# Two stacked transformer blocks on one core: the additions after the first down-projection in another order, and the low parts of the mixers' outputs 128 bytes further

## The chip, the cores and the metric
The kernel runs on one core of a Trainium2 chip. The metric is the device time in microseconds of one execution. Before the change the median of three runs is 984.97 us (984.92 to 984.98).

## The reference, cut to what matters
A sequence of 256 tokens of width 1024 goes through three layers in float32. In each, `h = h + mixer(rmsnorm(h))`, then `h = h + mlp(rmsnorm(h))`:

```
block 1, layer 0: mixer_ab  (attention on chosen keys | gated linear attention) -> 1024 columns, @ w_out_ab
                  mlp: square(relu(n @ w_up)) @ w_down,   w_up 1024x4096, w_down 4096x1024
block 1, layer 1: mixer_c   (stick-breaking attention, 8 heads of 128) -> 1024 columns, @ w_out_c
                  mlp of the same shapes
block 2:          16 meta tokens ahead of the 256; two gated branches, merged @ w_out;
                  gelu(a) * v of a convolved up-projection (2 x 2816 columns), @ w_down
```

rmsnorm divides each token's row by its root mean square and multiplies by a gain per column.

## The kernel before, in words
**Products in two parts.** Every large product is made of three matmuls on TensorE (helper `mm3`, lines 665 to 667): high x high, high x low, low x high. The high part is the value rounded to float32r, the low part is what is left. In the profile's names `whi`, `wlo` are the parts of a weight tile, `nhl` holds both parts of the normed tokens, `chi`, `clo` those of a mixer's output (`catT` in the code), `f`, `g`, `e` the areas with the parts of the three hidden layers, `mhi`, `mlo` those of block 2's merged branches and later of its normed tokens (`MG`). In a row as `bank<-whi,chi` the first name is the operand that is streamed through the array, the second is the one that is loaded into it.

**Weight tiles.** The weights come as 156 tiles, most of 128 x 2048 float32 (1 MB), in the order of use. For each tile i four steps run: SyncE issues its DMA into `raw` (slot i mod 3) when the low part of tile i-3 is made; ScalarE makes `whi` (line 1186, `hi(i)`) when the last matmul that read tile i-3 has ended; VectorE makes `wlo` (line 1750, `lo(i)`), for some tiles together with GpSimd (line 2422), each one half; then the matmuls may read it. Around the end of the first down-projection (tiles 35 to 50, `DOWN[0]` = 35) the tiles from 50 on are wholly VectorE's. Tiles 51 and 52 are the first two of the next layer's projection (`C0` = 51).

**Order of work.** Each engine has its own program, written out by hand in one order, with semaphores between the engines. An engine that waits lets nothing of its own program past.

**A projection back to tokens** (`out_tok`; s = 0 and 2 for the mixers, s = 1 and 3 for the first two MLPs) fills four PSUM banks: j = 2*tt + c, where tt is the half of the tokens and c the half of the columns. The loaded operand is the mixer's output or the hidden layer, the streamed one the weights, 512 columns a matmul. In the last tile the banks are finished one after the other in the order 0, 2, 1, 3, six matmuls each; ahead of bank 3 TensorE does `half_turn(t, 0)`: it transposes columns 0 to 511 of `h` (eight transposes, line 693), for which it waits until banks 0 and 2 have been added into `h`. VectorE's `add_out(s, j)` adds bank j into `h` once bank j is full; for s = 1 it is line 2035, since the MLP's row scale is applied there. Before the change VectorE first makes every low part up to tile 52 and then runs `out_h`: adds banks 0, 2, 1, makes the low parts of the transposed `h` (`half_turn`, line 1758, four instructions, after ScalarE's high parts, line 1194), adds bank 3. The next projection's first matmul needs the first of these four.

**Places in SBUF.** Tensors lie one behind the other in each partition, each rounded up to whole lines of 128 bytes: `raw`, `whi`, `wlo` (three each), `h`, `nhl`, `xn`, `clo`, `vec`, `cst`, `tri_sb`, small ones, and then the areas `a`, `f`, `g`, `c`, `b`, `e`, which share one room. `chi` and `mhi` lie on `xn`, `mlo` on `clo`. `xn` takes 8320 bytes, 32.5 times 256, so `clo` and `mlo` start 128 bytes off `chi` and `mhi` modulo 256. `whi`, `wlo`, `h`, `nhl`, `chi` start at the same place modulo 256 as one another; the high and the low part inside `f`, `g` and `e` do so too. `o_xn` and `o_clo` are the addresses of `xn` and `clo`, `place[0]` is the next free one.

Of the kernel before, what the change touches and what calls it, by code (L numbers as in the profile page):

```python
# [54 lines left out]
LINE = 128  # L55
# [169 lines left out]
UP, DOWN = (19, 67), (35, 83)  # L225
# [178 lines left out]
def block_kernel(nc, W, V, C, DL, CM, TRI, X, MT, WG, GP, OUT):  # L404
    ctx = ExitStack()
    with ctx:
# [3 lines left out]
        place = [base]  # L410
# [5 lines left out]
        def sb(name, n, dt=F32):  # L416
            off = place[0]
            place[0] += whole_lines(4 * n)
            return at(name, n, off, dt)
# [34 lines left out]
        o_xn = place[0]  # L454
        xn_ = sb("xn", 8 * N2)
        xn = xn_[:, 0:2 * D].rearrange("p (t n) -> p t n", t=2)
        o_clo = place[0]
        clo_ = sb("clo", 8 * S, F32R)
        place[0] = o_clo + whole_lines(8 * N2 * 4)
        catT = Pair(at("chi", 8 * S, o_xn, F32R), clo_).view("p (k t) -> p k t", k=8)  # L460
# [1276 lines left out]
        def vector_program(dve):  # L1737
# [3 lines left out]
            def lo(i):  # L1741
                j, m = i % NSLOT, cuts[i]
                if i < 2:
                    for c in range(4):
                        on.wait_ge(*s_hi01.at(i, c))
                        s = slice(c * 512, c * 512 + 512)
                        dve.tensor_tensor(wlo[j][:, s], raw[j][:, s], whi[j][:, s].bitcast(F32), ALU.subtract).then_inc(s_lo01.up(i, c))  # L1747
                    return
                on.wait_ge(*s_hi.at(i))
                dve.tensor_tensor(wlo[j][:, 0:m], raw[j][:, 0:m], whi[j][:, 0:m].bitcast(F32), ALU.subtract).then_inc(s_lod.up(i))  # L1750

            def evac_turn(t, q, dst):
                u = use["tr", t, q]
                on.wait_ge(*s_nhi.at(t, 2 * q + 1))
                for kk in range(2):
                    k = 2 * q + kk
                    o = dst[:, k, :]
                    dve.scalar_tensor_tensor(out=o.lo, in0=u.t[:, kk * 256:kk * 256 + 256], scalar=vcol(GAIN[t], k),  # L1758
                                             in1=o.hi.bitcast(F32), op0=ALU.mult,
                                             op1=ALU.subtract).then_inc(s_nlo.up(t, q) if kk == 0 else u.free if t < 4 else s_nodd.up(q))  # L1760

            def half_turn(t, c):
                for q in (2 * c, 2 * c + 1):
                    evac_turn(t, q, nTa if t < 4 else nT2[:, :, META:L2])
# [261 lines left out]
            def add_out(s, j, factor=None):  # L2026
                u = use["out", s, j]
                tt, c = j // 2, j % 2
                o = h[:, tt, c * 512:c * 512 + 512]
                on.wait_ge(*u.done(0 if j < 3 else (4, 16, 4, 16)[s] - 1))  # L2030
                if factor is None:
                    dve.tensor_tensor(o, o, u.t[:, :], ALU.add).then_inc(u.free)
                else:
                    on.wait_ge(*s_stat.at(factor, 2))
                    dve.scalar_tensor_tensor(out=o, in0=u.t[:, :], scalar=stats[factor][3][:, tt:tt + 1], in1=o,
                                             op0=ALU.mult, op1=ALU.add).then_inc(u.free)

            def out_h(s, factor, turn):
                for j in (0, 2, 1):
                    add_out(s, j, factor)  # L2040
                if turn:
                    half_turn(turn, 0)
                add_out(s, 3, factor)

            def mlp(l, t):
                def rest(m):
                    o, x = FFP[l][:, m * 512:m * 512 + 512], SQR[l][m % 2]
                    on.wait_ge(*s_ffhi.at(l, m))
                    dve.tensor_tensor(x, x, x, ALU.mult).then_inc(own.up())
                    on.wait_ge(*own.last())  # L2050
                    dve.tensor_tensor(o.lo, x, o.hi.bitcast(F32), ALU.subtract).then_inc(s_fflo.up(l, m))

                def joined(m, c):
                    u = use["up", l, m, c]
                    on.wait_ge(*s_half.at(l, m, c))
                    dve.tensor_tensor(SQR[l][m % 2][:, c * 256:c * 256 + 256], u.t[:, 0:256], HALVES[l][:, c * 256:c * 256 + 256],
                                      ALU.add).then_inc(u.free)

                for m in range(16):
                    if m:  # L2060
                        joined(m - 1, 1)
                    lo(UP[l] + m + 2)
                    if m == 0:
                        half_turn(t, 1)
                    joined(m, 0)
                    if m:
                        rest(m - 1)
                    if l == 1 and m == 6:
                        on.wait_ge(*s_mr.at(0))
                        dve.tensor_scalar(mnorm, meta, small[0:META, 9:10], None, ALU.mult).then_inc(s_mn.up(0))  # L2070
                joined(15, 1)
                rest(15)
# [4 lines left out]
                lo(OUT_AB + it + 2)  # L2077
            out_h(0, None, 1)
            mlp(0, 1)
            for it in range(16):  # L2080
                lo(DOWN[0] + it + 2)
            out_h(1, 1, 2)

# [397 lines left out]
        @block.vector  # L2483
        def _(eng):
            vector_program(eng)
# [124 lines left out]
```

## Time and profile before
| | |
|---|---|
| median of three runs | 984.97 us |
| profiled execution | 984.89 us |
| its span, first to last instruction | 983.1 us |
| TensorE (PE) busy | 971.7 us, 99% |
| VectorE (DVE) busy | 611.0 us, 62% |
| ScalarE (ACT) busy | 553.4 us, 56% |
| GpSimd (POOL) busy | 130.3 us, 13% |
| granted TensorE clock, mean | 0.998 |

PE counts a matmul from its start to its modelled end, and matmuls overlap, so two kernels may both show PE at 99% and still put their matmuls out at another pace: the distance from one matmul's start to the next is what counts. PEld is the load of the stationary operand, which runs beside the matmul ahead of it.

### The profile page before, as it was taken

What the parts mean: (1) busy time and instruction counts of PE and PEld (TensorE: products, weight loads), DVE (VectorE), ACT (ScalarE), POOL (GpSimd) and SP (SyncE); (2) the same over time, 40 slices, a digit from 0 to 9 for tenths busy, and PEclk for the clock granted to TensorE, in tenths of its full rate; (3) what the DMA queues carried; (4) which work ended last, traced back from release to release, by engine and by line L of the source; (5) the groups of instructions that cost most, each with busy time, mean ns of one, the idle gap of its engine ahead of it and who ended that gap; (6) DMA issues with size and microseconds to landing.
All of it is one profiled execution on the core that took longest, in us unless ns stands there. A gap on an engine that the chain in (4) does not pass through costs nothing.

```text
span 983.1 us, 14080 instructions
## 1 busy us (share of the span) xinstructions
PE 971.7 (99%) x5806; PEld 858.0 (87%) x5806; DVE 611.0 (62%) x894; ACT 553.4 (56%) x832; POOL 130.3 (13%) x44
## 2 busy tenths in 40 slices
PE   9999999999999999999999999999999999999997
PEld 7888888888888788888888888899999999999885
DVE  4997956777312554547777312376547689888643
ACT  6676347666433577846766433544454587665532
POOL 0011041000665000011000666300000000000000
PEclk9999999999999999999999999999999999999999
DMA  8454224555555543335545555464443535555541
GB/s 335 175 178 165 86 86 172 191 195 176 195 186 196 190 167 134 129 133 177 207 171 198 184 178 211 142 215 153 153 166 130 214 118 205 185 198 175 188 155 43
DMA packets 24804, 168.46 MB, mean 171 GB/s; under 512 B 2781, under 2 KB 3092, under 8 KB 4900
## 3 DMA queue, kind: packets, MB, share of 16 engines
q1 hardware_dynamic: 24452, 167.22, 47.2%
q8 instruction: 46, 0.75, 0.3%
q10 hardware_dynamic: 288, 0.33, 0.1%
q14 instruction: 18, 0.15, 0.1%
HBM read 166.49 MB, written 1.05 MB: 170 GB/s over the span
## 4 chain that ended last, share of the span: by engine, by line
PE 95%; ACT 2%; DVE 1%; DMA 1%; issue 0%; SPq 0%; DVEq 0%; ACTq 0%
PE bank L665 23%; PE bank L666 23%; PE bank L667 23%; PE bank L747 12%; PE bank L751 6%; PE bank L883 2%; PE bank L693 1%; DMA raw<-w_stream 1%; ACT whi L1186 1%; DVE wlo L1750 0%; PE bank L851 0%; PE bank L900 0%; PE bank L1094 0%; PE bank L993 0%; PE bank L1078 0%
## 5 line engine op out<-in xcount | busy, mean ns | idle before, releaser
L1750 DVE TENSOR_TENSOR wlo<-raw,whi 128x2048 fp32r<-128x2048 f32 (+2 forms) x152 | 310.7, 2045 | 266.0 <-ACT whi L1186 265.8
L1186 ACT ACTIVATE whi<-raw 128x2048 fp32r<-128x2048 f32 (+1 forms) x154 | 293.0, 1903 | 151.7 <-PE bank L667 148.9
L2422 POOL TENSOR_TENSOR wlo<-raw,whi 128x1024 fp32r<-128x1024 f32 (+1 forms) x37 | 129.1, 3493 | 496.0 <-ACT whi L1186 488.6
L747 PE MATMUL bank<-nhl,whi 128*128 128x512 f32 x512 | 130.4, 395 | 0.0
L667 PE MATMUL bank<-mhi,wlo 128*128 128x258 f32 x384 | 108.9, 284 | 0.0
L665 PE MATMUL bank<-mhi,whi 128*128 128x258 f32 x384 | 108.7, 283 | 0.0
L747 PEld LDWEIGHTS bank<-nhl,whi 128*128 128x128 f32 x512 | 92.2, 189 | 18.7 <-DVE nhl L1758 1.6
L666 PE MATMUL bank<-mlo,whi 128*128 128x258 f32 x384 | 108.3, 282 | 0.0
L665 PE MATMUL bank<-nhl,whi 128*128 128x258 f32 (+3 forms) x320 | 92.9, 290 | 0.0
L666 PE MATMUL bank<-nhl,whi 128*128 128x258 f32 (+3 forms) x320 | 91.3, 285 | 0.0
L667 PE MATMUL bank<-nhl,wlo 128*128 128x258 f32 (+3 forms) x320 | 90.5, 283 | 0.0
L665 PE MATMUL bank<-whi,nhl 128*128 128x512 f32 x192 | 76.9, 400 | 0.6 <-DVE wlo L1747 0.6
L667 PE MATMUL bank<-whi,nhl 128*128 128x512 f32 x192 | 74.9, 390 | 0.0
L666 PE MATMUL bank<-wlo,nhl 128*128 128x512 f32 x192 | 74.8, 390 | 0.0
L751 PEld LDWEIGHTS bank<-nhl,wlo 128*128 128x128 f32 x512 | 69.8, 190 | 5.0
L666 PEld LDWEIGHTS bank<-mlo,whi 128*128 128x128 f32 x384 | 72.8, 190 | 0.0
L667 PEld LDWEIGHTS bank<-mhi,wlo 128*128 128x128 f32 x384 | 72.5, 189 | 0.0
L665 PEld LDWEIGHTS bank<-mhi,whi 128*128 128x128 f32 x384 | 72.4, 189 | 0.1
L751 PE MATMUL bank<-nhl,wlo 128*128 128x256 f32 x512 | 71.4, 282 | 0.0
L665 PEld LDWEIGHTS bank<-nhl,whi 128*128 128x128 f32 (+1 forms) x320 | 60.4, 189 | 3.1 <-issue 2.9
L666 PEld LDWEIGHTS bank<-nhl,whi 128*128 128x128 f32 (+1 forms) x320 | 60.0, 188 | 0.2
L667 PEld LDWEIGHTS bank<-nhl,wlo 128*128 128x128 f32 (+1 forms) x320 | 60.1, 188 | 0.0
(298 smaller groups left out, 1757.9 us busy)
## 6 DMA issues: line engine op xcount, KB each, us to landing
raw<-w_stream SPq DMA_DIRECT2D x154, 1024.0 KB, 4.8
cst<-consts SPq DMA_DIRECT2D x1, 1200.0 KB, 11.6
h<-x_rows SPq DMA_DIRECT2D x4, 256.0 KB, 5.4
raw<-w_stream SPq DMA_DIRECT2D x2, 512.0 KB, 6.5
out_rows<-e SPq DMA_DIRECT2D x4, 256.0 KB, 2.1
e<-g_post SPq DMA_DIRECT2D x1, 512.0 KB, 3.7
raw<-w_stream SPq DMA_DIRECT2D x1, 352.0 KB, 9.5
b<-consts_x SPq DMA_DIRECT2D x1, 272.0 KB
```

What stands on the lines that cost most here:

```text
L665: pe.matmul(out, lhsT.hi, rhs.hi, start=start, stop=False)
L666: pe.matmul(out, lhsT.hi, rhs.lo, start=False, stop=False)
L667: return pe.matmul(out, lhsT.lo, rhs.hi, start=False, stop=stop)
L693: x = pe.transpose(u.t[:, kk * 256 + tt * P:kk * 256 + tt * P + P], h[:, tt, k * P:k * P + P], ident)
L747: return pe.matmul(us[c].t[:, :], w[:, k, c * P:c * P + P].hi, nboth[:, k, :], start=k == 0, stop=k == 7)
L751: pe.matmul(us[c].t[:, 0:256], w[:, k, c * P:c * P + P].lo, nTa[:, k, :].hi, start=False, stop=False)
L883: x = pe.matmul(u.t[:, i * P:i * P + P], kx, qx, start=True, stop=True)
L1186: act.activation(whi[j][:, 0:n], raw[j][:, 0:n], ACT.Copy).then_inc(s_hi.up(i))
L1750: dve.tensor_tensor(wlo[j][:, 0:m], raw[j][:, 0:m], whi[j][:, 0:m].bitcast(F32), ALU.subtract).then_inc(s_lod.up(i))
L2422: pool.tensor_tensor(wlo[j][:, m:n], raw[j][:, m:n], whi[j][:, m:n].bitcast(F32), ALU.subtract).then_inc(s_lop.up(i))
```

## The change
There are two edits. First, whole lines are added ahead of `clo` so that it lies at the same place modulo 256 as `xn` (and `chi`); `clo`, `mlo` and everything placed behind them move up by 128 bytes. Second, in VectorE's program, after the low part of tile 51, banks 0 and 2 are added first, then comes the low part of tile 52 (`DOWN[0] + 17`), then bank 1, the four low parts of the transposed `h`, and bank 3. No instruction is added or removed on any engine.

```
-        o_clo = place[0]
+        o_clo = place[0] = place[0] + (place[0] - o_xn) % (2 * LINE)
...
-            for it in range(16):
+            for it in range(15):
                 lo(DOWN[0] + it + 2)
-            out_h(1, 1, 2)
+            add_out(1, 0, 1)
+            add_out(1, 2, 1)
+            lo(DOWN[0] + 17)
+            add_out(1, 1, 1)
+            half_turn(2, 0)
+            add_out(1, 3, 1)
```

## Rows read from the trace of the kernel before

**Rows 1.** The page's parts 1 and 2: TensorE's busy time, its granted clock by slice.
```profile
PE 971.7 (99%) x5806; PEld 858.0 (87%) x5806; DVE 611.0 (62%) x894; ACT 553.4 (56%) x832; POOL 130.3 (13%) x44
...
PEclk9999999999999999999999999999999999999999
```
**Rows 2.** The view of waits from 330 us on, TensorE: us in total, times, longest.
```profile
PE bank L693 <- DVE h L2035: 1.1, 1, 1.1
```
**Rows 3.** The timeline, end of the first down-projection: start us, us, engine, line.
```profile
326.92 1.92 ACT L1186 ACTIVATE whi<-raw 128x2048 fp32r<-128x2048 f32 x1 [3.52 <-PE bank L667]
...
327.79 0.39 PE L667 MATMUL bank<-whi,f 128*128 128x512 f32 x1
...
328.86 2.29 DVE L1750 TENSOR_TENSOR wlo<-raw,whi 128x2048 fp32r<-128x2048 f32 x1 [3.15 <-ACT whi L1186]
...
329.15 0.39 PE L667 MATMUL bank<-whi,f 128*128 128x512 f32 x1
...
330.51 0.39 PE L667 MATMUL bank<-whi,f 128*128 128x512 f32 x1
331.07 2.06 DVE L2035 SCALAR_TENSOR_TENSOR h<-bank,rows,h 128x512 f32<-128x512 f32 x3
331.18 0.33 SPq L2440 DMA_DIRECT2D raw<-w_stream  x1
331.96 1.23 PE L693 MATMUL bank<-vec,h 128*128 128x128 f32 x8 [1.07 <-DVE h L2035]
332.94 0.48 PE L665 MATMUL bank<-whi,f 128*128 128x512 f32 x1
333.01 1.57 ACT L1194 ACTIVATE nhl<-bank,vec 128x256 fp32r<-128x256 f32 x4 [4.17 <-PE bank L693]
...
333.88 1.66 DVE L1758 SCALAR_TENSOR_TENSOR nhl<-bank,vec,nhl 128x256 fp32r<-128x256 f32 x4 [0.75 <-ACT nhl L1194]
...
334.51 0.47 PE L665 MATMUL bank<-whi,nhl 128*128 128x512 f32 x1
...
342.47 1.90 ACT L1186 ACTIVATE whi<-raw 128x2048 fp32r<-128x2048 f32 x1
```
**Rows 4.** The page's part 6: the weight tiles' DMAs, us from issue to landing.
```profile
raw<-w_stream SPq DMA_DIRECT2D x154, 1024.0 KB, 4.8
```
**Rows 5.** The timeline at the second mixer's projection, whose transposes had nothing to wait for.
```profile
444.60 0.40 PE L667 MATMUL bank<-whi,clo 128*128 128x512 f32 x1
444.84 1.17 PE L693 MATMUL bank<-vec,h 128*128 128x128 f32 x8
445.77 0.47 PE L665 MATMUL bank<-whi,chi 128*128 128x512 f32 x1
```
**Rows 6.** The timeline, two undisturbed runs of 48 matmuls: first start, and the 49th.
```profile
138.94 0.39 PE L665 MATMUL bank<-whi,chi 128*128 128x512 f32 x1
...
150.04 0.39 PE L665 MATMUL bank<-whi,chi 128*128 128x512 f32 x1
...
247.09 0.39 PE L665 MATMUL bank<-whi,f 128*128 128x512 f32 x1
...
257.98 0.39 PE L665 MATMUL bank<-whi,f 128*128 128x512 f32 x1
```
**Rows 7.** The timeline in block 2, 24 matmuls of 258 columns each: first start, the 25th.
```profile
820.18 0.28 PE L665 MATMUL bank<-mhi,whi 128*128 128x258 f32 x1
...
823.07 0.28 PE L665 MATMUL bank<-mhi,whi 128*128 128x258 f32 x1
...
655.04 0.28 PE L665 MATMUL bank<-nhl,whi 128*128 128x258 f32 x1
...
657.95 0.28 PE L665 MATMUL bank<-nhl,whi 128*128 128x258 f32 x1
```
**Rows 8.** The views of lines 983 and 976: duration ns min/median/max, first and last start us.
```profile
L983 PE MATMUL bank<-c,tri_sb x16: 377/378/454, 376.8 to 419.8; 128*128 128x256 f32 x16
...
L976 PE MATMUL bank<-c,c x16: 377/378/382, 367.2 to 409.6; 128*128 128x256 f32 x16
```

## The prediction
> **What bounds the kernel now.** I read the page's part 1 first: TensorE is busy for 971.7 of 983.1 us, and part 2 shows its clock at the full level of 2.4 GHz in all slices [rows 1]. So the time is that of TensorE's stream, and it changes in two ways only: by moments in which TensorE stands, and by the distance from one matmul's start to the next. For the first I read the view of waits, filtered for TensorE behind 330 us. Its largest entry is one wait of 1.1 us, of the transposes of `h` for VectorE's addition, line 2035 [rows 2]. That is the place the second edit touches. For the second I read timelines of undisturbed stretches and divided the time between two starts by the number of matmuls between them.
>
> **The order of the additions.** What the reader is to see in [rows 3] is a chain. The last tile's banks finish six matmuls at a time: bank 0 with the matmul at 327.79 (ends 328.18), bank 2 with that at 329.15 (ends 329.54), bank 1 with that at 330.51. VectorE, idle for 3.15 us until then, starts the low part of tile 52 at 328.86, as soon as ScalarE's high part is done, and so comes to the additions at 331.07 only, though both that the transposes need could have been made by 330.3. TensorE would have gone on at 330.51 + 0.23 = 330.74 and goes on at 331.96, 1.22 us late. The eight transposes then take 0.98 us to the next matmul (332.94 - 331.96); where nothing held them they took 0.93 (445.77 - 444.84) [rows 5]. After bank 3's six matmuls the next projection starts at 334.51, 1.57 us after 332.94. Behind it the end of the chain is again VectorE's: its four L1758 start at 333.88, and 0.63 us later, at 334.51, comes the first matmul that reads their result.
>
> With the new order, by the same durations, VectorE goes so:
> - Bank 0 is added from 328.2 to 328.95 in time that was idle.
> - Bank 2 is added from 329.63, 0.09 us after the modelled end. That delay is ScalarE's at 326.92: the matmul it waited for started at 327.79 - 6 x 0.227 = 326.43 and ended at 326.82. Additions in a row are (2.06 - 0.74)/2 = 0.66 us apart, so the low part of tile 52 starts at 330.29. Its successor followed 2.21 us after its start (331.07 - 328.86), so bank 1 is added from 332.50, and the L1758 may start at 333.16.
> - TensorE transposes from 330.74 to 331.67 without a wait, does bank 3's matmuls, and is ready for the next projection at 331.67 + 1.5 = 333.2. ScalarE's high parts (four in 1.57 us, from some 0.07 us after the transposes) are over by 333.4, the first two by 332.6, so line 1758 doesn't wait for them.
> - The first matmul of the projection comes at 333.16 + 0.63 = 333.79. TensorE stands for 0.6 us there: that is the wait that takes the place of the one removed.
>
> So this part gives 334.51 - 333.79 = 0.72 us. As ends I keep 0 (the wait turns up whole at the new place) and 1.3 us (the low part and bank 1 hide entirely, and TensorE goes on at 333.2: 334.51 - 333.2). I take 0.72 because every step of it has a row.
>
> What is moved behind this: the low part of tile 52 ends 1.4 us later. Queued behind it are bank 1, the L1758 and bank 3 on VectorE, counted above. The first reader of tile 52 is the second half of the projection, over 24 matmuls x 0.227 = 5.4 us after 333.8, and so it is covered. On SyncE the DMA into the same raw slot (tile 55) is issued behind it, at 332.6 in place of 331.18; with 4.8 us to landing [rows 4] it is there at 337.4. ScalarE has still to make the high parts of tiles 53 and 54 ahead of it, and the one of 54 starts at 342.47 [rows 3], so 5 us cover it. Bank 3's addition, the high part of tile 53 (it waits for bank 3's last matmul, 333.4 in place of 334.68) and the second set of transposes all come earlier. I see no later wait that a start 0.7 us earlier would lengthen: the engines that TensorE waits for in the next stage are themselves fed by TensorE.
>
> **The place of `clo`.** Here the rows show an effect of place alone. In the first mixer's projection 48 matmuls, alternately `chi`, `chi`, `clo` as loaded operand, take 150.04 - 138.94 = 11.10 us, 231.3 ns each. In the first down-projection, the same shapes in the same order, with high and low part at the same place modulo 256, 48 take 257.98 - 247.09 = 10.89 us, 226.9 ns each [rows 6]. The difference is 13 ns for each group of three. The two mixers' projections have 64 such groups, or 192 matmuls: 64 x 13 = 0.84 us at most. Behind each of six breaks (other work between the tiles) some ten matmuls run unevenly in both kinds, so I count 42 whole groups, 0.55 us, and 0.15 for the rest: 0.70 us. Ends: 0 and 0.84.
>
> The shift also moves `mlo`, which is streamed and not loaded. There 24 matmuls of 258 columns take 823.07 - 820.18 = 2.89 us although `mhi` and `mlo` differ by 128; with `nhl`, whose parts differ by 64 modulo 256, 24 take 657.95 - 655.04 = 2.91 us [rows 7]. So there is no sign of a penalty to be taken away, and a small one could come: 48 such blocks (1152 matmuls) x 0.02 = 1.0 us if they become like `nhl`. The groups of three inside the block are between 0.35 and 0.37 us apart around 0.361, which bounds 384 groups at -4.2 and +3.5 us. I take +0.2 us, nearer to none than to `nhl`, and keep +1.0 in the range. The areas behind move as a whole, and between their own parts nothing changes; I cost that at nothing, with the third rival as its price.
>
> The Trainium skill has a rule against this part: SBUF — State Buffer, section Specifications (TRN2), gives SBUF lines of 16 bytes, with a penalty for each crossing into a new one, and the section Operand start alignment of the same page asks for a multiple of the element size and says of it "This is about legality, not speed". A shift of 128 bytes changes neither. By that rule the place of `clo` is worth nothing and only the order counts. The trace does not agree so far, since [rows 6] differ by 4.4 ns a matmul with nothing else different that I can find.
>
> **The sum.** -0.72 - 0.70 + 0.2 = -1.2 us. The profiled execution took 984.89 us (span 983.1 and 1.8 around it), which gives 983.7. The median of the runs is 984.97, 0.08 above it; I say 983.7.
>
> **The rivals.**
> - *Place doesn't matter* (22%). The slow pace of `chi`/`clo` comes from their distance in some larger unit, or from something I don't see. For it: a distance of 8448 bytes is 256 off modulo 512 or 1024, while the fast pairs that I know lie at multiples of 1024. Against: [rows 6]. Then only the order counts: 984.97 - 0.72 = 984.2.
> - *The streamed operand likes it* (12%). The groups inside a block range from 0.35 to 0.37 us, so the place of a streamed operand does something; if `mlo` in step with `mhi` brings a third of the bound, 1.4 us, the time is 984.97 - 1.4 - 1.4 = 982.2. Against: `nhl` and `mhi` differ in place and hardly in pace.
> - *The loaded operand is slow at the other place* (5%, slower). The change puts `f`, `g` and `e` 128 bytes off `whi` modulo 256, where only `clo` was. If what costs is not the step between the two places but a load from the other one, then 384 + 384 + 264 = 1032 matmuls of the down-projections pay 13/2 = 6.5 ns each or more: +6.7 us, less 1.4, gives 990.3. It decides if an operand at the other place makes its matmul slow without an alternation. Against it: `tri_sb`, at the other place, has the same 378 ns as line 976's operand at the first one [rows 8], though that is plain float32.
> - *The wait just moves* (8%): VectorE's chain is no shorter, and the 1.2 us turn up at the new place; the alignment remains: 984.97 - 0.5 = 984.5.
>
> The forecast itself has 53%, with its own range from 983.0 to 984.4.
>
> **How the numbers follow.** A measurement of this kernel can tell about 0.2% from no change, so the limits are 983.0 and 986.9. Forecast, no effect of place and moved wait all lie within 0.2%, apart from a small tail of the forecast below 983.0; the streamed operand's case lies mostly below, the loaded one's above. Faster by over 0.2%: 0.15. Within: 0.79. Slower: 0.06. The range reaches down to a mild form of the second rival (0.6 us below the forecast's lower end) and up to the moved wait with the full +1.0 for `mlo`, nearly (984.5 + 0.6, since +0.2 is in it and both at their worst are unlikely): 982.4 to 985.1. It leaves out the loaded one's case and the rest of the second rival.
>
> **What would show it.** The order: the transposes start within 0.3 us of the matmul of bank 1, the wait for line 2035 is gone from the view of waits, and a new one of about 0.6 us stands before the first matmul of `nhl` at 333.8. The place of `clo`: 48 matmuls of the mixers' projections take 10.9 us, not 11.1, and the median duration of `whi,clo` is that of `whi,f`. The streamed operand: a block of 24 with `mlo` takes between 2.87 and 2.92 us. It would be wrong if the down-projections' matmuls are no longer 227 ns apart, or if TensorE waits 1.2 us or more before the next projection.

## The result and the profile after
The changed kernel takes 988.72 us (median of five, 988.61 to 989.34), the kernel before 984.94 in the same measurement: a ratio of 1.004, 95% interval 1.0029 to 1.005. It is slower by 3.8 us, where 1.2 us faster were forecast. The profiled execution took 988.87 us, its span is 987.1. Three single executions among all the runs below were disturbed (1608, 2477 and 4992 us) and count in no ratio; the one of 2477 us is the profiled one of `e5_base`, so of that run the time alone is used.

Nearly the same busy shares hide this: TensorE is at 99% in both. The change shows when the timeline is cut at the starts of the down-projections. These are rows of the kernel before (start us, duration us), the first matmuls of the three hidden layers, the first behind the second one, and the last matmul of all:
```profile
245.03 0.40 PE L665 MATMUL bank<-whi,f 128*128 128x512 f32 x1
...
539.12 0.50 PE L665 MATMUL bank<-whi,g 128*128 128x512 f32 x1
...
627.64 0.36 PE L665 MATMUL bank<-nhl,whi 128*128 128x272 f32 x1
...
915.95 0.40 PE L665 MATMUL bank<-whi,e 128*128 128x512 f32 x1
...
975.59 0.39 PE L667 MATMUL bank<-whi,e 128*128 128x512 f32 x1
```
The same in the kernel after:
```profile
245.05 0.39 PE L665 MATMUL bank<-whi,f 128*128 128x512 f32 x1
...
540.14 0.50 PE L665 MATMUL bank<-whi,g 128*128 128x512 f32 x1
...
630.69 0.36 PE L665 MATMUL bank<-nhl,whi 128*128 128x272 f32 x1
...
918.51 0.41 PE L665 MATMUL bank<-whi,e 128*128 128x512 f32 x1
...
979.64 0.39 PE L667 MATMUL bank<-whi,e 128*128 128x512 f32 x1
```
With 334.51 of before [rows 3] and 335.84 of after (below), the stretches are:

| stretch | before | after | difference |
|---|---|---|---|
| up to the first down-projection | 245.03 | 245.05 | +0.02 |
| first down-projection (`f`) and the end the order touches | 89.48 | 90.79 | +1.31 |
| second block's mixer and up-projection | 204.61 | 204.30 | -0.31 |
| second down-projection (`g`) | 88.52 | 90.55 | +2.03 |
| all up to the third (`e`) | 288.31 | 287.82 | -0.49 |
| third down-projection (`e`) | 59.64 | 61.13 | +1.49 |

The loss is in the three down-projections, and the rest together gains 0.8 us. The first of them loses less only because the new order gives back 0.82 us at its end (see below): without that the three lose 2.1, 2.0 and 1.5 us, which goes with the number of their matmuls (384, 384, 264). The pace of the matmuls says why. Again two runs of 48 in the timeline of after, the first start and the 49th; they answer to [rows 6]:
```profile
139.14 0.39 PE L665 MATMUL bank<-whi,chi 128*128 128x512 f32 x1
...
150.02 0.39 PE L665 MATMUL bank<-whi,chi 128*128 128x512 f32 x1
...
247.14 0.39 PE L665 MATMUL bank<-whi,f 128*128 128x512 f32 x1
...
258.29 0.39 PE L665 MATMUL bank<-whi,f 128*128 128x512 f32 x1
```
`chi` and `clo` went from 231.3 to 226.7 ns a matmul, as forecast. `f` went from 226.9 to 232.3 ns. If all 1032 matmuls of the three lose as much, that is 5.6 us. The view by tile shows the same in the durations (ns min/median/max), which were 389 in the median for `e` before:
```profile
L665 PE MATMUL bank<-whi,e x88: 390/393/405, 918.5 to 979.2; 128*128 128x512 f32 x88
```
The streamed `mlo` took no harm; this block of 24 answers to [rows 7] and takes 2.88 us (2.89 before). Over all 48 blocks the median went from 2.880 to 2.873 us, and together they take 0.2 us less:
```profile
822.62 0.29 PE L665 MATMUL bank<-mhi,whi 128*128 128x258 f32 x1
...
825.50 0.28 PE L665 MATMUL bank<-mhi,whi 128*128 128x258 f32 x1
```
The end of the first down-projection, timeline of after, answers to [rows 3]:
```profile
332.36 2.28 DVE L1750 TENSOR_TENSOR wlo<-raw,whi 128x2048 fp32r<-128x2048 f32 x1
...
332.66 0.40 PE L667 MATMUL bank<-whi,f 128*128 128x512 f32 x1
...
332.89 1.03 PE L693 MATMUL bank<-vec,h 128*128 128x128 f32 x8
...
333.68 0.48 PE L665 MATMUL bank<-whi,f 128*128 128x512 f32 x1
...
335.22 1.65 DVE L1758 SCALAR_TENSOR_TENSOR nhl<-bank,vec,nhl 128x256 fp32r<-128x256 f32 x4
...
335.84 0.47 PE L665 MATMUL bank<-whi,nhl 128*128 128x512 f32 x1 [0.52 <-DVE nhl L1758]
```
The transposes start 0.23 us after bank 1's last matmul, one matmul's pace, and no longer wait. The next projection's first matmul comes 3.18 us after that matmul (335.84 - 332.66), before it was 4.00 (334.51 - 330.51). The view of waits has the exchange: the 1.1 us of [rows 2] became
```profile
PE bank L665 <- DVE nhl L1758: 0.5, 1, 0.5
```

### The profile page after: what moved, and what is told of

Same layout as the page of the kernel before. It is cut to its first block, busy times and chain, and to the rows that moved or that the text cites. A ratio compares the mean times of both kernels' runs of the same rounds, so it can differ in the third digit from the quotient of the medians.

```text
span 987.1 us, 14080 instructions
## 1 busy us (share of the span) xinstructions
PE 976.3 (99%) x5806; PEld 858.4 (87%) x5806; DVE 610.7 (62%) x894; ACT 553.8 (56%) x832; POOL 130.7 (13%) x44
## 4 chain that ended last, share of the span: by engine, by line
PE 95%; DVE 2%; ACT 2%; DMA 1%; issue 0%; SPq 0%; DVEq 0%
PE bank L665 23%; PE bank L666 23%; PE bank L667 23%; PE bank L747 12%; PE bank L751 6%; PE bank L883 2%; DMA raw<-w_stream 1%; PE bank L693 1%; DVE wlo L1750 1%; PE bank L851 0%; PE bank L900 0%; PE bank L1094 0%; ACT whi L1186 0%; PE bank L993 0%; PE bank L1078 0%; PE bank L919 0%
## 5 line engine op out<-in xcount | busy, mean ns | idle before, releaser
L665 PE MATMUL bank<-mhi,whi 128*128 128x258 f32 x384 | 108.7, 283 | 0.0
L665 PE MATMUL bank<-nhl,whi 128*128 128x258 f32 (+3 forms) x320 | 92.8, 290 | 0.0
L665 PE MATMUL bank<-whi,nhl 128*128 128x512 f32 x192 | 76.9, 400 | 1.1 <-DVE wlo L1747 0.6
L665 PEld LDWEIGHTS bank<-mhi,whi 128*128 128x128 f32 x384 | 72.6, 189 | 0.3
L665 PEld LDWEIGHTS bank<-nhl,whi 128*128 128x128 f32 (+1 forms) x320 | 60.3, 189 | 3.0 <-issue 2.9
```

What stands on the lines that cost most here:

```text
L665: pe.matmul(out, lhsT.hi, rhs.hi, start=start, stop=False)
```

## The experiments
The theory was: a matmul of 512 streamed columns is about 5 ns slower when its loaded operand lies off the streamed one modulo 256 (in step means that both start at the same place modulo 256 bytes). The rivals: the order costs; places other than the areas' cost; the loaded operand's own address counts and not the relation.

**The order alone** (`e1_order`): only the second edit of the change.
```
-            for it in range(16):
+            for it in range(15):
                 lo(DOWN[0] + it + 2)
-            out_h(1, 1, 2)
+            add_out(1, 0, 1)
+            add_out(1, 2, 1)
+            lo(DOWN[0] + 17)
+            add_out(1, 1, 1)
+            half_turn(2, 0)
+            add_out(1, 3, 1)
```


> The kernel before with the new order of the additions alone; every place as before. Theory (the place of f, g and e costs, the order gains): 984.2 us, 0.7 below before, f matmuls 227 ns apart, and one wait of about 0.6 us ahead of the next projection in place of the one of 1.1 us. Rival (the new order itself costs, by its late low part of tile 52 and the later DMA): at or above 985.5 us.


Measured: 984.01 us against 984.87, ratio 0.9991 (0.9982 to 1.0). The interval touches 1, but its executions (983.85 to 984.34) all lie below those of before (984.56 to 985.22), and the spans of the two profiles differ by about as much, 0.9 us; the wait is now `L665 <- DVE nhl L1758` with 0.6 us. The order gains.

**The place alone** (`e2_place`): only the first edit.
```
-        o_clo = place[0]
+        o_clo = place[0] = place[0] + (place[0] - o_xn) % (2 * LINE)
```


> The kernel before with clo and all behind it 128 bytes further; order as before. Theory: 989.5 us: 1032 matmuls of the three down-projections 232 ns apart in place of 227 (+5.5 us), 128 of the mixers' matmuls faster (-0.7). Rival (the order carries the loss): 984.3 us.


Measured: 989.27 us, ratio 1.0045 (1.0031 to 1.006). The whole loss is in this edit, and its largest wait is the one of before:
```profile
PE bank L693 <- DVE h L2035: 1.0, 1, 1.0
```

**The whole change, with the areas put back** (`e3_both_room`): both edits and
```
+        place[0] += 128
         room = place[0]
```


> The changed kernel with 128 more bytes ahead of the areas, so that f, g and e lie again as whi modulo 256, while clo stays in step with chi. Theory: f, g, e and clo all 227 ns: 983.5 us, below both kernels. Rival (not the places of the areas but those of vec, cst or mlo cost): stays near 988.7 us.


Measured: 983.32 us, ratio 0.9986 (0.9977 to 0.9995), 1.55 us below before. `clo`, `mlo`, `vec` and `cst` are where the change puts them, `f`, `g`, `e` are back in step with the weights, and both kinds are fast. The view by tile has
```profile
L666 PE MATMUL bank<-whi,f x128: 389/389/476, 244.9 to 332.1; 128*128 128x512 f32 x128
...
L668 PE MATMUL bank<-whi,clo x64: 388/389/398, 130.7 to 446.0; 128*128 128x512 f32 x64
```

**The areas alone** (`e4_room`): the kernel before with that one line.


> The kernel before with 128 more bytes ahead of the areas alone; clo, mlo, vec and cst as before, order as before. Theory: 232 ns for f, g, e, +5.5 us: 990.4 us. Rival (vec, cst, mlo or clo carry it): 985.0 us.


Measured: 990.60 us, ratio 1.0061 (1.0048 to 1.0074): 5.73 us for 1032 matmuls, 5.6 ns each. The line moves the other areas (`a`, `c`, `b`) too, but the trace puts the loss where the theory has it: from its first to its last matmul `f` takes 2.0 us longer than before, `g` 2.0 and `e` 1.7, together all of it. With the one above this settles what the loss hangs on. (At the same address `e` loses 1.7 us here and 1.5 in `after` and `e2_place`; why is open.)

**Everything 128 bytes further, weights too** (`e5_base`).
```
-        place = [base]
+        place = [base + 128]
```


> The kernel before with every tensor 128 bytes further, weights too, so that all relations stay. Theory (the relation between loaded and streamed operand counts): 984.9 us, f at 227 ns. Rival (the address of the loaded operand counts by itself): f, g, e at 232 ns, +5.5 us, and the projections' nhl too, +3 us: 990 to 993 us.


Measured: 984.85 us against 984.93, ratio 1.0 (0.9991 to 1.0009). Moving everything by 128 bytes costs nothing: what counts is not the address by itself but the relation.

**All but the weights 128 bytes further** (`e6_weights`).
```
+        place[0] += 128
         h = sb("h", 2 * D).rearrange("p (t n) -> p t n", t=2)
```


> The kernel before with 128 more bytes behind the weight tiles, so that h, nhl, chi, f, g and e all lie off the weights. Theory: f, g, e (1032), nhl (576) and chi (128) as loaded operand at 232 ns, clo (64) at 227: +9 us, 994 us. If the relation counts the other way round too (weights loaded, nhl of 512 columns streamed, 512 matmuls), +2.7 more: 996.5 us. Rival (only the areas' places matter): 990.4 us.


Measured: 994.59 us, ratio 1.0099 (1.0085 to 1.0113), +9.7 us. The forecast without the other way round was 994, with it 996.5; it lies nearer to the first. The up-projections, weights loaded and 512 columns of `nhl` streamed, did lose some: their matmuls (view of lines; busy us, mean ns) were 130.4 us before and are
```profile
L748 PE MATMUL bank<-nhl,whi 128*128 128x512 f32 x512 | 131.6, 397 | 0.0
```
From start to start they are 236.4 ns apart in the mean, before 233.9, which is 1.3 us for 512, about half of what a down-projection's matmul loses. (Before, in step, they were already slower than the down-projections' matmuls: a median duration of 393 ns and 231 from start to start, against 389 and 227.) But not all comes out as expected: `clo`, now in step, stays slow, with 397 ns in the median.

**64 bytes instead of 128** (`e7_room64`): `place[0] += 64` ahead of the areas.


> The kernel before with 64 more bytes ahead of the areas. If the cost grows with the distance up to 128: f, g, e near 229.5 ns, 987.7 us. If only the half of 256 in which an operand starts counts: 64 is in the same half, 984.9 us. If any offset costs the whole: 990.5 us.


Measured: 991.23 us, ratio 1.0065 (1.0051 to 1.0079), +6.3 us. Half the distance costs as much or a little more, so at 64 and 128 bytes the cost does not grow with the distance; being out of step costs the whole.

**256 bytes** (`e8_room256`): `place[0] += 256` ahead of the areas.


> The kernel before with 256 more bytes ahead of the areas. Theory (a period of 256 bytes): 984.9 us, f at 227 ns. Rival (a larger period, or any move of the areas costs): above 986.5 us.


Measured: 984.98 us against 984.93, ratio 1.0001 (0.9991 to 1.001). Moving the areas by itself costs nothing, and 256 bytes bring the old pace back, where 64 and 128 did not.

**High part in step, low part off** (`e9_mid`): 128 bytes between the two parts inside `f`, `g` and `e`.
```
-            def pair(self, n):
-                return Pair(self(n, F32R), self(n, F32R))
+            def pair(self, n, mid=0):
+                hi = self(n, F32R)
+                self.at += mid
+                return Pair(hi, self(n, F32R))
...
+            FFP.append(A.pair(32 * S, 128))
...
+        FF2 = A.pair(22 * S, 128).view("p (k t) -> p k t", k=22)
```


> The kernel before with 128 more bytes between the high and the low part inside f, g and e: high in step with the weights, low off. Theory (a matmul is slow when the operand it uses, or the one loaded beside it for the next, is off): line 665 at 227 ns, 666 at 232, 667 at 234, as chi and clo have it; 344 groups x 13 ns = +4.5 us: 989.4 us. Rival (only the matmul whose own operand is off is slow): one in three, +1.9 us: 986.8 us.


Measured: 989.09 us, ratio 1.0043 (1.0029 to 1.0056), +4.2 us. `f` now has the pattern of `chi` and `clo` before the change, 389, 396 and 397 ns. The first matmul of a group is at full pace; the second, which has its own operand in step and only the off part loaded beside it, is slow, and so is the third:
```profile
L667 PE MATMUL bank<-whi,f x128: 389/389/476, 244.9 to 335.2; 128*128 128x512 f32 x128
...
L668 PE MATMUL bank<-wlo,f x128: 392/396/398, 245.1 to 335.4; 128*128 128x512 f32 x128
...
L669 PE MATMUL bank<-whi,f x128: 393/397/401, 245.4 to 335.6; 128*128 128x512 f32 x128
```
So the load of the next operand counts as well as the one in use, and the rival at 986.8 is out.

**High part off, low part in step** (`e11_mid_room`): this and the areas 128 bytes further.


> As the one above, and the areas 128 bytes further: high part off, low part in step. Theory: all three lines slow, 16 to 17 ns a group, +5.6 us: 990.6 us. Rival (own operand only): two in three slow, +3.8 us: 988.7 us.


Measured: 991.28 us, ratio 1.0064 (1.0051 to 1.0078), +6.4 us, a little beyond the theory's 990.6. All three lines are slow, the third too, whose own operand is in step:
```profile
L668 PE MATMUL bank<-whi,f x128: 392/393/474, 245.0 to 336.0; 128*128 128x512 f32 x128
...
L669 PE MATMUL bank<-wlo,f x128: 387/395/395, 245.2 to 336.3; 128*128 128x512 f32 x128
...
L670 PE MATMUL bank<-whi,f x128: 397/397/398, 245.4 to 336.5; 128*128 128x512 f32 x128
```
That also explains why `clo` stayed slow when all but the weights moved: `chi` is loaded beside it.

**Both places in step, and tile 52's low part last** (`e10_best`), next to the third experiment's kernel once more (`e12_again`).
Against the kernel after the change:
```
+        place[0] += 128
         room = place[0]
...
             add_out(1, 2, 1)
-            lo(DOWN[0] + 17)
             add_out(1, 1, 1)
             half_turn(2, 0)
             add_out(1, 3, 1)
+            lo(DOWN[0] + 17)
```


> clo in step with chi, the areas back in step with the weights, and the low part of tile 52 behind all of the additions and the low parts of the transposed h. Theory: the wait of 0.5 us ahead of the next projection is gone: 982.8 us. Rival (the low part, now ready only about 338 us, or the DMA behind it, makes a new wait in the projection's second half): 983.3 us or more.

> clo in step with chi, the areas back in step, the order of the changed kernel: the same kernel as e3, here beside e10 on one chip. 983.3 us; the difference to e10 is the place of the low part of tile 52 alone.


Measured: 983.20 us (982.98 to 983.65) and 983.40 (983.20 to 983.60), ratios to before 0.9982 (0.9973 to 0.9991) and 0.9985 (0.9976 to 0.9993). Both beat both kernels. Of the 0.6 us of wait that went, the median keeps 0.2, which their overlapping runs don't establish. The trace shows 0.23 of the rest, where the rival had it: VectorE makes the low parts of tiles 52 and 53 back to back and comes late to the second half of `nhl`. (The profiled execution of `e10_best` is its slowest, 983.65 us; it loses 0.4 us against that of `e12_again` at 27.8 us, in a stage that the edit doesn't touch.) Timeline of `e10_best`:
```profile
334.98 2.28 DVE L1751 TENSOR_TENSOR wlo<-raw,whi 128x2048 fp32r<-128x2048 f32 x1
...
337.24 2.28 DVE L1751 TENSOR_TENSOR wlo<-raw,whi 128x2048 fp32r<-128x2048 f32 x1
...
339.44 1.26 DVE L1759 SCALAR_TENSOR_TENSOR nhl<-bank,vec,nhl 128x256 fp32r<-128x256 f32 x3
...
339.61 0.39 PE L668 MATMUL bank<-whi,nhl 128*128 128x512 f32 x1
...
340.07 0.47 PE L666 MATMUL bank<-whi,nhl 128*128 128x512 f32 x1
```
The last two starts are 0.46 us apart and not 0.23, and the second comes 0.63 us behind the start of the L1759, as in [rows 3].

## Why the prediction was wrong
- *The order of the additions, -0.72 us*: right. Alone it gave -0.86 us. The wait that remains was put at 0.6 us and is 0.5 to 0.6. That the later low part of tile 52 and the DMA behind it are covered held too.
- *The place of `clo`, -0.70 us*: right. From the trace before to the trace after, the matmuls with `chi` and `clo` take 0.70 us less. The runs have it with `mlo` in it only: with `f`, `g`, `e` kept in step, the first edit is worth 984.01 - 983.32 = 0.69 us.
- *`mlo`, +0.2 us*: the wrong way by a little. The 48 blocks together take 0.2 us less in the kernel after, and 0.3 less from `e1_order` to `e3_both_room`; the rival in which the streamed operand gains 1.4 us did not happen either. The prediction compared the places of `mhi` and `mlo` with each other. What counts in the down-projections is the place against the weights, and there hardly anything changed: a row of either takes 258 x 4 = 1032 bytes, 8 more than four times 256, so row k lies 8k bytes off the weights, for `mlo` 8k + 128 before the change. Only `mlo`'s row 0 came into step, and its matmuls stay 121 ns apart from the next.
- *The areas behind, costed at nothing*: this is the step that failed, and it outweighs the rest. It said that "between their own parts nothing changes", which is true and not what counts. `f`, `g` and `e` are loaded while `whi` and `wlo` are streamed, and those did not move. The runs put +5.7 us in its place (`e4_room`). The prediction's own sign of being wrong came up: the down-projections' matmuls are no longer 227 ns apart.
- *The rival "the loaded operand is slow at the other place"* was the case. Its price was 6.5 ns a matmul, half of the 13 ns of a group, and it measured 5.6; that is 1.0 of the 1.6 us between its 990.3 and the measured 988.72, and the order and `mlo` have most of the rest. `e5_base` narrows it: what costs is not the other place as such, but a place other than the streamed operand's.
- *Why it got 5%*: on the argument that `tri_sb` at the other place costs line 983 nothing [rows 8]. The place was read wrongly. From `xn` to `tri_sb` there are 65 + 65 + 21 + 75 = 226 lines of 128 bytes (`xn`, `clo`, `vec`, `cst`), an even number, so `tri_sb` lies as `xn` and the weights do modulo 256, and as `c`: both rows were in step, and the argument had nothing under it. Had it been off, the row could not have shown it either. In `e4_room` `c` has moved off `tri_sb`, and the line, which is plain float32, keeps its 378 ns and its 215 ns from start to start:
```profile
L984 PE MATMUL bank<-c,tri_sb x16: 377/378/455, 378.9 to 422.0; 128*128 128x256 f32 x16
```
- *The row that could show it* was in the trace of before all along: with one of three operands off, two of three matmuls were slow, as these medians show beside the 389 ns of the first line of a group.
```profile
L665 PE MATMUL bank<-whi,chi x64: 389/389/478, 130.1 to 446.5; 128*128 128x512 f32 x64
...
L666 PE MATMUL bank<-wlo,chi x64: 387/396/398, 130.4 to 446.8; 128*128 128x512 f32 x64
...
L667 PE MATMUL bank<-whi,clo x64: 390/397/403, 130.6 to 447.0; 128*128 128x512 f32 x64
```
The alternation of places was read as what costs, and the pattern also fitted a cost of being off. A candidate that costs 1032 matmuls needed a better reason to be left at 5%.
- *Sum*: -0.86 for the order, -0.69 for `clo` and `mlo` and +5.73 for the areas is +4.2; measured is +3.8. Of the 0.4 us between, 0.2 is in `e`, which loses 1.5 us here and 1.7 in `e4_room`; the rest is not assigned, since the effects were each taken from another pair of kernels.

The Trainium skill's SBUF — State Buffer, section Specifications (TRN2), has lines of 16 bytes, with a penalty for crossing into a new one. By that rule moves by whole lines, which change no crossing, are free. The runs agree for 256 bytes (984.98 us against 984.93) and for everything moved together (984.85), and not for 64 bytes, four such lines, which cost 6.3 us; the measurement decides.

## What to carry to other kernels
Before padding one tensor, list everything that lies behind it and moves with it, and for each the operands it meets in one instruction: pad both sides, so that only the one moves. For float32r matmuls of 512 columns, keep the loaded operand, both of its parts, in step with the streamed one modulo 256 bytes. Before a row is used as evidence on a place, add up the places of both of its operands: here that sum was what the 5% hung on. When a slow and a fast case differ in two ways at once (off, and alternating), price both readings on every instruction the change touches.

## What the hardware showed that was not expected
- A matmul of 512 float32r columns takes 227 ns from start to start with the loaded operand in step with the streamed one modulo 256 bytes, and 232 to 235 ns (in the mean over a line's matmuls) out of step, at 64 bytes as at 128. Moving all tensors together changes nothing (984.85 us against 984.93). That holds with the weights streamed; with the weights loaded (line 747) it is 233.9 ns in step and 236.4 out of step (`e6_weights`), in the mean.
- The load of the next operand counts as the operand in use does (`e9_mid`, `e11_mid_room`). Why an offset costs these 5 ns stays open; other offsets, such as 16 or 32 bytes, were not tried.
- For matmuls of 258 columns, weights loaded, nothing is shown about being in step, since all rows but the first lie off the weights in every kernel. In the mean over the blocks their starts follow each other after 114 to 125 ns, by the position in the block; moving `mlo` changes which positions are fast, and a block's 2.880 us by 0.007 only.
- Plain float32 matmuls of 256 columns (line 983) showed no cost of being off: 378 ns in step and 378 off by 128 bytes (`e4_room`). Where `tri_sb` itself has moved it is 380, in step (`after`) as off (`e3_both_room`).
